# One TensorE loop for experts 4 to 30: the overflow branch moved from behind expert 15 to behind expert 3

## The chip, the cores and the metric

The kernel runs on one core of one Trainium2 chip. The metric is the device time of one execution in microseconds (us), as the median of several runs. The engines are called TensorE (PE), VectorE (DVE), ScalarE (ACT), GpSimd (POOL) and SyncE (SP). SyncE here only issues transfers and waits.

## The reference

One step of a hybrid decoder layer on 280 token rows (16 meta tokens, 256 prompt tokens, 8 sampled ones), all in float32. It has two sub-layers. The first mixes tokens (RG-LRU and gated linear attention) and isn't touched here. The second is a mixture of experts: 32 experts, of which each token takes 4. This is what the change is about:

```python
logits = u @ w_router + b_router
top_val, top_idx = lax.top_k(logits, TOP_K)          # 4 of 32
gates = softmax(top_val)
# for each expert e, on the rows routed to it:
gu = xb @ w_gu[e] + b_gu[e]                           # w_gu[e]: 1024 x 2048
gate = minimum(gu[:, :1024], 7.0)
lin = clip(gu[:, 1024:], -7.0, 7.0)
act = (lin + 1.0) * gate * sigmoid(1.702 * gate)
y += row_weight * (act @ w_down[e] + b_down[e])       # w_down[e]: 1024 x 1024
```

Each expert has 8.39 MB of `w_gu` and 4.19 MB of `w_down`, 12.58 MB in all and 402.7 MB for the 32. A final RMSNorm follows.

## The kernel before

**A pass.** Each expert is one pass (`body(i)` on every engine) over at most S = 64 rows that were routed to it. On TensorE a pass `i` does, in this order: the gate and up matmuls `gu(i, e, k0, k1)` in four quarters (L1560), with the scatter of the results of expert `i - 2` behind the second quarter (`scatter`, L1602) and the gather of the rows of expert `i + 1` behind the third (`gather`, L1532); the down matmuls of expert `i - 1` (`dn`, L1579); and a few transposes for what comes next (`turn_rows` L1539, `turn_weights` L1619, `turn_gu` L1626). VectorE and ScalarE do the activation of the expert before, copy results out of PSUM and add them to `yacc`.

**Counters.** The quarters increment `used0`, `used2`, `used4` and `used6` when their weights have been read, the four parts of `dn` increment `used8` to `used11`. `x_turned` is incremented when the rows of the next expert have been transposed, at the end of a pass.

**The weight queue.** All weights go through one ring of nine buffers of 2.1 MB each. SyncE issues the loads in order. For an expert from the fourth on there are two loads of `w_gu` of 4096 KB (`gate_linear_four`, for the pieces `GU[0]` and `GU[2]`) and the `w_down` of the expert before, as one load of 4096 KB (`down_whole`) or, for experts 0 to 2 and each third one after, as two of 2048 KB (`down`). Before each load it waits on two things: that the previous load of the same piece has landed (`landed`) and that TensorE has read what lies in the buffer (`used...`). For experts 3 to 15 this is `fours_ahead`: the first load waits for `used9 >= e - 2`, the second for `used0 >= e`. For experts 16 to 31 it is `fours_behind_rows`, which is the same but for the first load, which waits for `x_turned >= i`. `down_ahead` follows both. These loads run through the helper at L321 and have that line in the profile.

**Overflow.** If an expert gets more than 64 rows, more passes are needed. VectorE works out `flag` early, before the first pass ends. TensorE, VectorE, ScalarE and SyncE each read it once (`value_load`) and have a loop over EXTRA = 129 more passes under an `If`. With these inputs the flag is 0 and the loop is jumped over. Which expert the branch stands behind is `SPLIT`:

```python
    SPLIT = NE // 2        # 16
    BIAS = 2
```

TensorE runs experts 0 to 3 unrolled, a loop of 4 rounds with 3 unrolled passes each (experts 4 to 15), the flag and the jump over the overflow loop (also 3 unrolled passes long), a loop of 5 rounds with 3 passes (experts 16 to 30), and `finish` with expert 31. VectorE and ScalarE do the same through `passes`, with loops of one pass. SyncE's program is unrolled for all experts, but for the overflow loop. GpSimd has no part in the experts.

Of the kernel before, what the change touches and what calls it, by code (L numbers as in the profile page):

```python
# [5 lines left out]
def hybrid_layer_kernel(nc, A, O):  # L6
# [20 lines left out]
    NE, FF = A["w_gu"].shape[1], A["w_down"].shape[2]  # L27
# [21 lines left out]
    NSLOT = 18  # L49
    EXTRA = NV - NE + 1  # L50
    GU = list(range(0, 8, 2))
    SPLIT = NE // 2
    BIAS = 2
    DN = list(range(8, 12))
    DOWN = DN[::2]
    QUADS = range(BIAS + 1, NE)

    ctx = ExitStack()
    with ctx:
        sems = {}  # L60

        def sem(name):

            if name not in sems:
                sems[name] = ctx.enter_context(nc.semaphore(name))
            return sems[name]
# [211 lines left out]
        def four_of(e, p):  # L278

            n = (e * 6 + 7 + p // 2) % (NSLOT // 2)  # L280
            return mem[:, n * 4096:(n + 2) * 4096]
# [5 lines left out]
        def split_down(e):  # L287

            return e <= BIAS or e % 3 == 0

        def second_halves(e):

            return sum(split_down(j) for j in range(e + 1))

        def both_of(e):

            n = (e * 6 + 8) % (NSLOT // 2)
            return mem[:, n * 4096:(n + 2) * 4096]
# [5 lines left out]
        def e_of(i):  # L304
            return i if isinstance(i, int) else i % NE
# [13 lines left out]
        def _(sp):  # L319
            def load(dst, src, name):  # L320
                sp.dma_start(dst, src).then_inc(sem(name), 16)  # L321
# [49 lines left out]
            def gate_linear(p, i, e):  # L371

                first, k = p - p % 4, p % 4
                src = A["w_gu"][0, bass.ds(e_of(i), 1), first * P:(first + 4) * P, :].rearrange("e (p k) n -> p (e k) n", p=P)
                load(pair_of(e, p).rearrange("p (k n) -> p k n", k=2), src[:, k:k + 2, :], f"piece_in{p}")

            def gate_linear_four(p, i, e):

                src = A["w_gu"][0, bass.ds(e_of(i), 1), p * P:(p + 4) * P, :].rearrange("e (p k) n -> p (e k) n", p=P)
                load(four_of(e, p).rearrange("p (k n) -> p k n", k=4), src, f"piece_in{p}")  # L380

            def down_rows_of(i):

                return A["w_down"][0, bass.ds(e_of(i), 1), :, :].rearrange("e (p k) n -> p (e k) n", p=P)

            def down(p, i, e):

                k = 2 * (p - 8)
                load(down_of(e, p).rearrange("p (k n) -> p k n", k=4), down_rows_of(i)[:, k:k + 4, :], f"piece_in{p}")

            def down_whole(i, e):

                load(both_of(e).rearrange("p (k n) -> p k n", k=KD), down_rows_of(i), f"piece_in{DN[0]}")

            def landed(p, n):

                sp.wait_ge(sem(f"piece_in{p}"), 16 * n)
# [8 lines left out]
            gate_linear(GU[3], 1, 1)  # L406
            down(DN[0], 0, 0)
            sp.wait_ge(sem("used0"), 1)
            down(DN[2], 0, 0)
            sp.wait_ge(sem("u2_ready"), 3)  # L410
# [3 lines left out]
            def down_ahead(i, e, triples=0):  # L414

                landed(DN[0], i - 1)
                if not split_down(e - 1):
                    sp.wait_ge(sem("used4"), i)
                    down_whole(i - 1, e - 1)
                    return  # L420
                sp.wait_ge(sem("used2"), i)
                down(DN[0], i - 1, e - 1)
                landed(DN[2], triples + second_halves(e - 2))
                sp.wait_ge(sem("used4"), i)
                down(DN[2], i - 1, e - 1)

            def fours_ahead(e):

                landed(GU[0], e)
                sp.wait_ge(sem("used9"), e - 2)  # L430
                gate_linear_four(GU[0], e, e)
                landed(GU[2], e)
                sp.wait_ge(sem("used0"), e)
                gate_linear_four(GU[2], e, e)
                down_ahead(e, e)

            def ahead(e):

                landed(GU[0], e)
                sp.wait_ge(sem("used2" if e == 2 else "used6"), 1 if e == 2 else e - 1)  # L440
                gate_linear(GU[0], e, e)
                landed(GU[1], e)
                sp.wait_ge(sem("used4" if e == 2 else "used9"), 1 if e == 2 else e - 2)
                gate_linear(GU[1], e, e)
                landed(GU[2], e)
                sp.wait_ge(sem("used6" if e == 2 else "used11"), 1 if e == 2 else e - 2)
                gate_linear(GU[2], e, e)
                landed(GU[3], e)
                sp.wait_ge(sem("used0"), e)
                gate_linear(GU[3], e, e)  # L450
                down_ahead(e, e)

            def fours_behind_rows(i, e, triples):

                landed(GU[0], i)
                sp.wait_ge(sem("x_turned"), i)
                gate_linear_four(GU[0], i, e)
                landed(GU[2], i)
                sp.wait_ge(sem("used0"), i)
                gate_linear_four(GU[2], i, e)  # L460
                down_ahead(i, e, triples)
# [12 lines left out]

            ahead(2)
            for e in range(QUADS[0], SPLIT):
                fours_ahead(e)
            sp.wait_ge(sem("flag_ready"), 1)
            over = sp.value_load(flag[0:1, 0:1], min_val=0, max_val=1)
            with sp.If(over):  # L480
                with sp.Fori(0, EXTRA // 3) as g:
                    for f in range(3):
                        in_turn(g * 3 + (SPLIT + f), SPLIT + f)
            more = over * EXTRA
            extra_triples = over * (EXTRA // 3)
            for e in range(SPLIT, NE):
                fours_behind_rows(more + e, e, extra_triples)
            sp.wait_ge(sem("scattered"), TC * (BIAS - 1))
            load(gfin, A["g_final"].rearrange("(a n) -> a n", a=1).broadcast_to([P, D]), "gfin_in")
            for w in range(4):  # L490
# [15 lines left out]
        def passes(eng, body, finish, after_bias=None):  # L506

            body(0)
            body(1)
            body(BIAS)  # L510
            if after_bias is not None:
                after_bias()
            with eng.Fori(BIAS + 1, SPLIT) as i:
                body(i)
            eng.wait_ge(sem("flag_ready"), 1)
            over = eng.value_load(flag[0:1, 0:1], min_val=0, max_val=1)
            with eng.If(over):
                with eng.Fori(SPLIT, SPLIT + EXTRA) as i:
                    body(i)
            more = over * EXTRA  # L520
            with eng.Fori(SPLIT, NE - 1) as i:
                body(i + more)
            finish(more + (NE - 1))
# [4 lines left out]
        def lags(i):  # L528

            n = i if isinstance(i, int) else NE  # L530
            return n >= 1, n >= 2
# [714 lines left out]
        def _(pe):  # L1246
# [358 lines left out]
            def scatter(i, e):  # L1605
# [3 lines left out]
                pe.wait_ge(sem("biased"), 2 * i)  # L1609
                if e == BIAS + 1:  # L1610
                    pe.wait_ge(sem("gd_ready"), 2)
# [23 lines left out]
            def body(i, e, triples=0):  # L1635
                do_j, do_m = lags(e)

                pe.wait_ge(sem("xT_ready"), i + 1)
                if do_j:
                    pe.wait_ge(sem("guS_ready"), i)  # L1640
                gu(i, e, 0, 2)
                gu(i, e, 2, 4)
                if do_m:
                    scatter(i, e)
                gu(i, e, 4, 6)
                if do_m:
                    pe.wait_ge(sem("added"), TC * (i - 2) + 2)
                gather(i + 1)
                gu(i, e, 6, 8)
                if do_j:  # L1650
                    pe.wait_ge(sem("act_ready"), i)
                    if do_m:
                        pe.wait_ge(sem("added"), TC * (i - 1))
                    for p in DN:
                        dn(i, e, p, actT, 4, triples + second_halves(e - 1))
                turn_rows(i + 1)
                if do_j:
                    turn_weights(i, 6)
                if e == BIAS:
                    turn_gates()  # L1660
                if not do_j:
                    pe.wait_ge(sem("flag_ready"), 1)
                turn_gu(i)
# [29 lines left out]
                pe.wait_ge(sem("sq_h"), len(nth_half) + 2)  # L1693
                pe.matmul(ps[:, 1, 0:1], same_row, ssq[:, 2:3], start=True, stop=True).then_inc(sem("last_sum"), 1)

            for e in range(BIAS + 2):
                body(e, e)
            with pe.Fori(0, (SPLIT - BIAS - 2) // 3) as g:
                for f in range(3):
                    body(g * 3 + (BIAS + 2 + f), BIAS + 2 + f, g * 1)  # L1700
            pe.wait_ge(sem("flag_ready"), 1)
            over = pe.value_load(flag[0:1, 0:1], min_val=0, max_val=1)
            with pe.If(over):
# [3 lines left out]
            more = over * EXTRA  # L1707
            extra_triples = over * (EXTRA // 3)
# [30 lines left out]
```

## Time and profile before

| | |
|---|---|
| median of 3 runs | 1085.46 us (1085.46 to 1085.59) |
| the profiled execution | 1085.73 us, span of its instructions 1084.0 us |
| TensorE matmul | 97% of the span busy, mean granted clock 0.995 |
| VectorE, ScalarE | 30% and 18% |
| moved by DMA | 425.59 MB, mean 393 GB/s |

The span is the time from the first to the last instruction on the core, and the little around it belongs to the launch. A view of the profile can be restricted to a window, counted in microseconds from the start of the span. In the window view there is one row per window: its length, the busy time and the number of instructions of each engine, then the granted clock of TensorE (1.00 is full speed), the mean busy share of the 16 DMA engines (which can be a little over 1 by the way packets fall on borders) and GB/s. The chain of waits is followed back from the last instruction, each step to what released it.

In the trace, expert 0 starts on TensorE at 162.54 us, expert 3 at 234.75, expert 4 at 265.48 and expert 16 at 605.98.

### The profile page before, as it was taken

To read this page: it belongs to the slowest core of one execution; us is meant where nothing else is said; L and a number is where in the kernel's file an instruction comes from. 1 tells how busy PE (TensorE), PEld (TensorE's weight loads), DVE (VectorE), ACT (ScalarE), POOL (GpSimd) and SP (SyncE) were. 2 spreads that over 40 slices of the span, in tenths; PEclk is the share of its full clock that TensorE was granted. 3 is DMA by queue.
4 is the path that set the end of the run, shared out by engine and by line. 5 is a ranking of instruction groups with operands and counts; after the bars stand their busy time and mean duration, and the time that the engine had idled before them with its cause. 6 is when DMAs were issued, how large, how long until landed. Compare 5 with 4: busy or idle time off the path is not lost.

```text
span 1084.0 us, 13426 instructions
## 1 busy us (share of the span) xinstructions
PE 1051.5 (97%) x5387; PEld 436.1 (40%) x5387; DVE 325.2 (30%) x660; ACT 193.8 (18%) x319; POOL 14.9 (1%) x39
## 2 busy tenths in 40 slices
PE   7999999999999999999999799999999999999996
PEld 5758573333333333333333233333333333333332
DVE  6854342212222222222222222222222222122234
ACT  3463332111111111111111011111111111110112
POOL 4100000000000000000000000000000000000000
PEclk9999999999999999999999899999999999999999
DMA  9751689999999999999999999999999999999993
GB/s 303 262 192 50 253 360 386 425 427 414 433 429 428 435 433 424 438 432 430 433 428 433 430 427 432 430 432 433 426 435 432 429 432 434 432 429 432 435 406 148
DMA packets 34586, 425.59 MB, mean 393 GB/s; under 512 B 5335, under 2 KB 12334, under 8 KB 19450
## 3 DMA queue, kind: packets, MB, share of 16 engines
q1 hardware_dynamic: 33816, 424.76, 93.2%
q8 instruction: 22, 0.36, 0.1%
q0 software_dynamic: 512, 0.26, 0.1%
q10 hardware_dynamic: 226, 0.13, 0.0%
q14 instruction: 10, 0.08, 0.0%
HBM read 422.82 MB, written 2.35 MB: 392 GB/s over the span
## 4 chain that ended last, share of the span: by engine, by line
PE 62%; DMA 36%; issue 1%; DVE 1%; ACT 0%; SPq 0%; ACTq 0%; DVEq 0%
DMA mem<-in_w_gu 35%; PE ps L1560 24%; PE ps L1579 12%; PE ps L1278 6%; PE ps L1532 4%; PE ps L1602 3%; PE ps L1437 3%; PE ps L1626 2%; PE ps L1324 1%; PE ps L1539 1%; DMA mem<-in_w_in 1%; PE ps L1586 1%; PE ps L1619 1%; PE ps L1462 0%; PE ps L1317 0%
## 5 line engine op out<-in xcount | busy, mean ns | idle before, releaser
L1560 PE MATMUL ps<-mem 128*64 128x512 f32 x2048 | 459.8, 597 | 13.3 <-issue 6.3
L1560 PEld LDWEIGHTS ps<-mem 128*64 128x64 f32 x2048 | 141.9, 137 | 288.6 <-issue 272.8
L1579 PE MATMUL ps<-mem 128*64 128x512 f32 x1024 | 226.0, 593 | 0.7
L1170 DVE TENSOR_TENSOR mem<-ps,bguT 128x512 f32<-128x512 f32 x64 | 41.2, 686 | 372.6 <-PE ps L1626 372.6
L1579 PEld LDWEIGHTS ps<-mem 128*64 128x64 f32 x1024 | 75.3, 137 | 145.1 <-issue 145.0
L1200 DVE TENSOR_TENSOR yacc<-ps,yacc 128x1024 f32<-128x1024 f32 x64 | 75.6, 1220 | 131.1 <-PE ps L1602 131.1
L752 ACT ACTIVATE mem<-ps 128x512 f32<-128x512 f32 x32 | 19.1, 597 | 385.6 <-PE ps L1532 384.7
L1532 PE MATMUL ps<-mem 128*64 128x512 f32 x372 | 85.1, 592 | 0.0
L1278 PE MATMUL ps<-mem 128*128 128x280 f32 x256 | 64.4, 410 | 2.1 <-DMA mem<-in_w_in 2.1
L1602 PE MATMUL ps<-mem 64*128 64x512 f32 x256 | 64.1, 616 | 1.7 <-ACT mem L817 0.9
L1152 DVE TENSOR_TENSOR mem<-slot_no,pos 128x192 f32<-128x192 f32 x32 | 11.5, 358 | 165.9 <-PE ps L1532 165.9
L1278 PEld LDWEIGHTS ps<-mem 128*128 128x128 f32 x256 | 49.2, 194 | 14.9 <-DMA mem<-in_w_in 2.4
L803 ACT ACTIVATE mem<-ps 128x512 f32<-128x512 f32 x31 | 18.5, 597 | 179.7 <-PE ps L1579 179.5
L796 ACT ACTIVATE mem<-ps 128x1024 f32<-128x1024 f32 x32 | 32.8, 1024 | 99.4 <-PE ps L1560 99.4
L1532 PEld LDWEIGHTS ps<-mem 128*64 128x64 f32 x372 | 26.7, 137 | 53.1 <-issue 53.1
L1602 PEld LDWEIGHTS ps<-mem 64*128 64x128 f32 x256 | 21.9, 186 | 42.3 <-issue 42.3
L781 ACT ACTIVATE mem<-mem 128x512 f32<-128x512 f32 x30 | 18.9, 630 | 96.7 <-DVE mem L1177 96.7
L1626 PE MATMUL ps<-ident,mem 128*128 128x128 f32 x256 | 33.8, 275 | 0.5 <-ACT mem L796 0.5
L1626 PEld LDWEIGHTS ps<-ident,mem 128*128 128x128 f32 x256 | 30.9, 191 | 1.5 <-ACT mem L796 0.8
L1437 PE MATMUL ps<-mem 128*128 128x512 f32 (+1 forms) x80 | 28.9, 512 | 0.0
L1539 PEld LDWEIGHTS ps<-ident,mem 128*128 128x128 f32 x128 | 17.9, 209 | 25.2 <-issue 25.2
L1184 DVE TENSOR_SCALAR mem<-slot_no,pos,gate 128x128 f32<-128x128 f32 x96 | 27.3, 341 | 1.3 <-PE ps L1619 1.3
(318 smaller groups left out, 517.4 us busy)
## 6 DMA issues: line engine op xcount, KB each, us to landing
mem<-in_w_gu SPq DMA_DIRECT2D x58, 4096.0 KB, 27.5
mem<-in_w_down SPq DMA_DIRECT2D x18, 4096.0 KB, 29.0
mem<-in_w_down SPq DMA_DIRECT2D x26, 2048.0 KB, 24.2
mem<-in_w_gu SPq DMA_DIRECT2D x12, 2048.0 KB, 12.6
mem<-in_w_in SPq DMA_DIRECT2D x5, 2048.0 KB, 16.2
mem<-in_w_out SPq DMA_DIRECT2D x1, 4096.0 KB, 14.0
mem<-in_w_down SPq DMA_DIRECT2D x4, 1024.0 KB, 21.5
mem<-in_state_gla SPq DMA_DIRECT2D x8, 128.0 KB, 2.5
```

What stands on the lines that cost most here:

```text
L796: act.activation(guS[:, :].rearrange("p (a n) -> p a n", a=2), ps[:, 0:2, :], ACT.Copy).then_inc(sem("guS_ready"), 1)
L1170: dve.tensor_tensor(hS[:, n, :].rearrange("p (k s) -> p k s", k=8), turned[:, n], bguT[:, 8 * n:8 * n + 8, bass.ds(e_of(i - 1), 1)].broadc ...
L1184: dve.tensor_scalar(Gm[:, c, :], slot_no[:, :], pos[:, c, bass.ds(i - 1, 1)], gate[:, c, bass.ds(e_of(i - 1), 1)], ALU.is_equal, ALU.mult) ...
L1200: dve.tensor_tensor(dst, ps[:, PAIR[c]:PAIR[c] + 2, :], dst, ALU.add).then_inc(sem("added"), 1)
L1278: last = pe.matmul(ps[:, bank_of(t), 0:NT], w(k), uT[:, k, :], start=(k == K_ORDER[0]), stop=(k == K_ORDER[-1]))
L1437: last = pe.matmul(ps[:, OUT_BANK[c, n], 0:(k1 - k0) * P], mixed(k)[:, c * P:c * P + P], wout[:, k, k0 * P:k1 * P], start=(k == 0), stop=( ...
L1532: last = pe.matmul(ps[S * w:S * w + S, 5, :], sel[:, c, :], u2[:, c, w * 512:(w + 1) * 512], start=(c == 0), stop=(c == TC - 1))
L1539: last = pe.transpose(ps[:, 5, q * P:(q + 1) * P], xr[:, q:4 * P:4], ident[:, :])
L1560: last = pe.matmul(ps[S * w:S * w + S, n, :], xT[:, k % 4, k // 4, :], weights[:, col:col + 512], start=(k == 0), stop=(k == KD - 1))
L1579: last = pe.matmul(ps[S * w:S * w + S, bank, :], acts[:, k, :], weights[:, col:col + 512], start=(k == 0), stop=(k == KD - 1))
L1602: last = pe.matmul(ps[:, PAIR[c] + n, :], weights[S * n:S * n + S, c * P:(c + 1) * P], values[S * n:S * n + S, :], start=start, stop=stop)
L1626: last = pe.transpose(ps[:, 2 + f // 4, (f % 4) * P:(f % 4 + 1) * P], guS[:, f:KD * P:KD], ident[:, :])
```

## The change

- `SPLIT` becomes `BIAS + 2`, that is 4. The flag is read, and the overflow loop jumped over, behind expert 3 instead of behind expert 15, on SyncE, TensorE, VectorE and ScalarE.
- TensorE's loop over experts 4 to 15 is gone. What was the loop over 16 to 30 now covers 4 to 30, in 9 rounds of 3.
- VectorE and ScalarE run expert 3 unrolled, and then one loop over 4 to 30.
- SyncE keeps the waits that it had for each expert: `fours_ahead` up to expert 15 and `fours_behind_rows` from 16. As the experts from 4 on now lie behind the branch, `fours_ahead` takes a pass number `i` that comes from a register, beside the expert's number `e`, and its first two waits are exchanged.

```diff
--- before.py
+++ after.py
@@ -49,8 +49,8 @@
     NSLOT = 18
     EXTRA = NV - NE + 1
     GU = list(range(0, 8, 2))
-    SPLIT = NE // 2
     BIAS = 2
+    SPLIT = BIAS + 2
     DN = list(range(8, 12))
     DOWN = DN[::2]
     QUADS = range(BIAS + 1, NE)
@@ -424,15 +424,15 @@
                 sp.wait_ge(sem("used4"), i)
                 down(DN[2], i - 1, e - 1)
 
-            def fours_ahead(e):
-
-                landed(GU[0], e)
-                sp.wait_ge(sem("used9"), e - 2)
-                gate_linear_four(GU[0], e, e)
-                landed(GU[2], e)
-                sp.wait_ge(sem("used0"), e)
-                gate_linear_four(GU[2], e, e)
-                down_ahead(e, e)
+            def fours_ahead(i, e, triples=0):
+
+                sp.wait_ge(sem("used9"), i - 2)
+                landed(GU[0], i)
+                gate_linear_four(GU[0], i, e)
+                landed(GU[2], i)
+                sp.wait_ge(sem("used0"), i)
+                gate_linear_four(GU[2], i, e)
+                down_ahead(i, e, triples)
 
             def ahead(e):
 
@@ -474,7 +474,7 @@
 
             ahead(2)
             for e in range(QUADS[0], SPLIT):
-                fours_ahead(e)
+                fours_ahead(e, e)
             sp.wait_ge(sem("flag_ready"), 1)
             over = sp.value_load(flag[0:1, 0:1], min_val=0, max_val=1)
             with sp.If(over):
@@ -484,7 +484,10 @@
             more = over * EXTRA
             extra_triples = over * (EXTRA // 3)
             for e in range(SPLIT, NE):
-                fours_behind_rows(more + e, e, extra_triples)
+                if e < NE // 2:
+                    fours_ahead(more + e, e, extra_triples)
+                else:
+                    fours_behind_rows(more + e, e, extra_triples)
             sp.wait_ge(sem("scattered"), TC * (BIAS - 1))
             load(gfin, A["g_final"].rearrange("(a n) -> a n", a=1).broadcast_to([P, D]), "gfin_in")
             for w in range(4):
@@ -510,8 +513,7 @@
             body(BIAS)
             if after_bias is not None:
                 after_bias()
-            with eng.Fori(BIAS + 1, SPLIT) as i:
-                body(i)
+            body(BIAS + 1)
             eng.wait_ge(sem("flag_ready"), 1)
             over = eng.value_load(flag[0:1, 0:1], min_val=0, max_val=1)
             with eng.If(over):
@@ -1693,11 +1695,8 @@
                 pe.wait_ge(sem("sq_h"), len(nth_half) + 2)
                 pe.matmul(ps[:, 1, 0:1], same_row, ssq[:, 2:3], start=True, stop=True).then_inc(sem("last_sum"), 1)
 
-            for e in range(BIAS + 2):
+            for e in range(SPLIT):
                 body(e, e)
-            with pe.Fori(0, (SPLIT - BIAS - 2) // 3) as g:
-                for f in range(3):
-                    body(g * 3 + (BIAS + 2 + f), BIAS + 2 + f, g * 1)
             pe.wait_ge(sem("flag_ready"), 1)
             over = pe.value_load(flag[0:1, 0:1], min_val=0, max_val=1)
             with pe.If(over):
```

## Rows read from the trace of the kernel before

**Rows 1.** The page: rate in 40 slices of 27.1 us; one load's landing.

```profile
GB/s 303 262 192 50 253 360 386 425 427 414 433 429 428 435 433 424 438 432 430 433 428 433 430 427 432 430 432 433 426 435 432 429 432 434 432 429 432 435 406 148
...
mem<-in_w_out SPq DMA_DIRECT2D x1, 4096.0 KB, 14.0
```

**Rows 2.** The chain of waits: start, us, what.

```profile
265.48 7.02 PE ps L1560 x32
...
599.72 6.25 issue
605.98 8.48 PE ps L1560 x32
...
663.15 3.61 PE ps L1560 x16
...
695.03 29.07 DMA mem<-in_w_gu
...
1044.88 7.09 PE ps L1560 x32
```

**Rows 3.** Busy time by window, from 271 us on.

```profile
271.00:325.00 54.00, 54.00 (x272) 19.81 (x270) 13.81 (x25) 7.63 (x12) 0.00 (x0) 1.00 1.01 432
595.00:649.00 54.00, 47.75 (x236) 17.61 (x234) 14.14 (x25) 6.01 (x10) 0.00 (x0) 0.94 1.01 430
811.00:1000.00 189.00, 182.88 (x906) 67.36 (x906) 46.11 (x82) 24.54 (x38) 0.00 (x0) 1.00 1.00 431
```

**Rows 4.** L321: issues in 250 to 252, 259 to 270, 598.7 to 612.

```profile
L321 SPq DMA_DIRECT2D mem<-in_w_down x1: 328/328/328, 250.8 to 250.8; - x1
...
DMA to landing us min/median/max: 13.1/13.1/13.1
...
L321 SPq DMA_DIRECT2D mem<-in_w_gu x2: 328/328/328, 260.2 to 269.2; - x2
...
DMA to landing us min/median/max: 15.2/15.6/15.9
...
L321 SPq DMA_DIRECT2D mem<-in_w_gu x2: 332/332/333, 598.8 to 611.3; - x2
...
DMA to landing us min/median/max: 25.3/26.7/28.1
```

**Rows 5.** Busy time in the window from 606 to 609 us.

```profile
606.00:609.00 3.00, 3.00 (x8) 1.00 (x10) 0.00 (x0) 0.00 (x0) 0.00 (x0) 0.53 1.02 431
```

**Rows 6.** Instruction packets in 244 to 600, then in 600 to 690 us.

```profile
q8 instruction: 5, 0.08, 0.1%
...
q8 instruction: 5, 0.08, 0.4%
```

**Rows 7.** The timeline of SyncE's issues: start, us, what.

```profile
213.68 6.40 SPq L321 DMA_DIRECT2D mem<-in_w_down  x2
229.18 0.33 SPq L321 DMA_DIRECT2D mem<-in_w_gu  x1
...
278.66 0.33 SPq L321 DMA_DIRECT2D mem<-in_w_down  x1
...
588.16 1.01 SPq L321 DMA_DIRECT2D mem<-in_w_down  x2
```

**Rows 8.** L321: issues at 154.0 and 154.4 us, then at 166.2.

```profile
L321 SPq DMA_DIRECT2D mem<-in_w_gu x1: 328/328/328, 154.0 to 154.0; - x1
L321 SPq DMA_DIRECT2D mem<-in_w_down x1: 434/434/434, 154.4 to 154.4; - x1
...
DMA to landing us min/median/max: 7.4/9.7/11.9
...
L321 SPq DMA_DIRECT2D mem<-in_w_down x1: 328/328/328, 166.2 to 166.2; - x1
...
DMA to landing us min/median/max: 8.8/8.8/8.8
```

**Rows 9.** Waits in 596 to 608 us: total, times, longest.

```profile
ACT mem L781 <- DVE mem L1177: 3.4, 1, 3.4
```

## The prediction

> **What bounds the kernel now.** I read the page first. Its slices show the DMA at 360 GB/s by 135 us, then 425 and 427, a dip to 414 in the tenth slice (244 to 271 us), and from there never under 424 until the slice in which the last weights land [rows 1]. TensorE is busy 97% too, so the page alone doesn't say which of the two sets the end.
>
> Next the chain of waits [rows 2]. Up to 663 us it runs through TensorE (an expert every 27.85 us, one with the gap at 599.72 excepted), then through transfers of `w_gu`, one every 29.1 us. The tempting reading is that TensorE is the bound until 663 us and that every microsecond taken from it there is a microsecond won. The windows say otherwise [rows 3]: from 271 us on, in the TensorE part of the chain as in the DMA part, the rate is 429 to 434 GB/s with a share of 1.00 or 1.01 (eleven windows, of which three are shown). An expert is 12.58 MB (4.19 MB in each of three loads), at 431 GB/s 29.2 us. The DMA has been the bottleneck since 271 us. TensorE, at 27.85 us, only eats up a lead of landed weights, 1.3 us of it per expert, and at 663 us the lead is gone. The end is therefore: the moment from which the DMA never runs dry, plus the bytes left, plus the tail of TensorE work after the last landing at 1044.88 us. A TensorE stall costs nothing if the transfers already issued outlast it; otherwise what the DMA loses is never given back.
>
> So the measure is the backlog: for each load, how long after its issue the load before it lands. From the issues and their times to landing [rows 4]: at 611.3 us the previous load (598.8 + 28.1) lands at 626.9, a backlog of 15.6 us. At 269.2 us it (260.2 + 15.2) lands at 275.4: 6.2 us. At 260.2 us it (250.8 + 13.1) lands at 263.9: 3.7 us.
>
> **What the change removes: the stall at expert 16.** Between experts 15 and 16 TensorE stands 6.25 us for "issue" [rows 2]. There the program reads the flag, jumps over the unused overflow loop and enters the second loop. After it the granted clock is at half speed (1.2 GHz instead of 2.4) until about 609 us, with the engine idle before [rows 5]; the first 32 matmuls take 8.48 us where those of expert 4 take 7.02 [rows 2]. In all, the quarter that lets SyncE issue the next `w_gu` load comes 611.3 - 599.72 = 11.6 us after the expert's start, at expert 4 269.2 - 265.48 = 3.7 us: a delay of 7.8 us (some 0.1 of it SyncE's register work). The backlog there is 15.6 us, delay included, and the load issued at 611.3 lands at 636.6, 9.7 us after its predecessor, the full rate. The window around it, 430 GB/s [rows 3], agrees. So the term for the removal is **0**; its cover is the backlog.
>
> **What it adds: the same stall at expert 4.** Today TensorE falls straight into the first loop there, with no gap: the chain has its matmuls from 265.48 us on with no "issue" ahead of them [rows 2]. After the change the flag read and the jump over three unrolled overflow bodies stand at this place. Would the code already be in the engine? Five instruction packets come in 244 to 600 us, for twelve experts, and five in 600 to 690, for three [rows 6]: the first loop's code stays in the engine after its first round, and the code past the jump doesn't come ahead of the jump. The code jumped over is as long as the loop, so the target is as far off at expert 4 as it was at 16. I take the same delay, 7.8 us. Bounds: nothing, if it is hidden, and 7.8 us as measured; between them 4.5 us, if the fetch takes only the 2.5 us of latency that a quiet DMA shows below, with 2 us for the clock and the rest.
>
> The Trainium skill (Runtime: NRT & Kernel Launch, "Instruction fetch mechanics") says that an engine streams code in 16 KiB blocks and that a taken branch to a block outside what it holds stalls for a fetch by DMA. The rows of packets agree. Under it the stall moves whole and the sum is as below.
>
> **What lies behind it.** Everything SyncE issues after 265 us waits on TensorE's counters: the second `w_gu` half of expert 5 at 269.2 waits for `used0`, the `w_down` load at 278.7 [rows 7] for `used4`. The first would come at 269.2 + 7.8 = 277.0. The DMA runs dry at 275.4. What a load costs on a dry queue I bound by rows. A 2 MB load issued at 154.0 into a quiet DMA lands after 7.4 us, one issued at 166.2, just as its predecessor (154.4 + 11.9) ends, after 8.8 us [rows 8]. Less 4.85 us for 2.1 MB at full rate that is 2.55 and 3.95 us of latency, so 12.3 to 13.7 us for 4.2 MB; `w_out`, alone in its time, took 14.0 [rows 1], and the load at 260.2, on a backlog of 3.7 us, even 15.2. I take 13.7, the row in which the queue runs dry just then as here. The landing moves from 285.1 to 277.0 + 13.7 = 290.7, **5.6 us** later. Floor: 4.2 (with 12.3); with the short stall of 4.5 us, 0.9 to 2.3. Ceiling: 7.1 (with 15.2). The next load, `w_down`, moves from 278.7 to 286.5, 4.2 us before 290.7, so it follows nearly without a gap. At that backlog the load at 260.2 lost 11.5 - 9.75 = 1.75 us, so up to 1.7 may come on top until the backlog has grown. After that the DMA is never dry again and the loss stays to the end.
>
> The Trainium skill (DMA: Bandwidth & Descriptors) puts the fixed cost of a transfer near 2 us. The rows here show 2.5 to 4.3; by the page's figure the term would be 277.0 + 11.7 - 285.1 = 3.6 us instead of 5.6, an estimate.
>
> **The rest.** SyncE's own branch moves to between 219.7, when the second `w_down` half is issued (the pair that begins at 213.68 and lasts 6.40), and 229.18 us, when it goes on [rows 7]: it stands 9.1 us for `used9` there. At expert 16 its branch fitted between the `w_down` issues that begin at 588.16 and end at 589.2, and the issue at 598.8, 9.6 us [rows 4, 7], without being seen. I take 0. Where it needs more than the 9.1, a backlog of at least 3.7 us (the thinnest, rows 4) covers the first part; what is beyond that is lost one for one, and I allow 3 us for it. ScalarE's branch lies in a wait of 3.4 us ended by VectorE's data [rows 9], VectorE's in a longer one: 0. If ScalarE's cover were gone, the excess would delay the activation, which TensorE wants only behind all its gate and up matmuls. The exchanged order of `used9` and the landed wait changes nothing, as both must hold: 0. Register values in twelve experts' waits and addresses: 0.1 us an issue, under a backlog of 6 us and more: 0. Unrolling expert 3 on ScalarE and VectorE: same work, same waits, 0.
>
> **Sum.** 0 + 5.6 + 0 = 5.6 us. The profiled execution took 1085.73 (span 1084.0), the median is 1085.46, so the sum on the former is 1091.3 and on the median **1091.1 us**, half a per cent slower.
>
> **Rivals.**
> (a) *The queue runs dry* as worked out: 1088.5 to 1093.2. For it: 6.2 us of backlog against 7.8 of delay. Chance 0.64.
> (b) *The stall is hidden or short.* A delay under some 4.5 us is absorbed but for 2 us, and the time is 1085.5 (1084.5 to 1087.5). For it: a DMA with little queued may bring the code faster than the full one at 600 us. Against it: the packets are there only after the jump in the one case shown. Chance 0.20.
> (c) *SyncE falls late as well.* From 9.1 us plus at least 3.7 of backlog on, each microsecond of its branch is one more on top of (a): with up to 3 of them 1091.1 to 1094.1. For it: its branch is only known to fit into 9.6 us at expert 16, where nothing would have shown a late issue of some microseconds, with 15.6 of backlog. Chance 0.08.
> (d) *Faster.* The chain is right to go through TensorE, and what counts is its time up to 663 us. The branch, now close behind the start of the loop code, costs no more than the fall into the loop does today: 7.8 us go and none comes back, 1085.5 - 7.8 = 1077.7. It decides only if the rate can rise above 431 GB/s once TensorE frees its buffers sooner. The windows of rows 3 speak against it, the backlog of 15.6 us too. Chance 0.08.
>
> **Numbers.** Within 0.2% (2.2 us) is what a measurement can't tell from no change. (a) and (c) lie outside it: slower 0.72; (b) 0.20; (d) 0.08. The likeliest case alone: 1088.5 to 1093.2. The range takes in (b) from 1085.2 and (a) to 1093.2; it leaves out (d), the worse part of (c) and a little of (b).
>
> **What the next profile would show.** A gap for "issue" of about 6 us on TensorE near 265 us, with a half clock behind it, and none near 600; instruction packets there and none later. The load that waits for `used0` of expert 4 is issued near 277 us and lands near 290.7. The window 250 to 290 us shows a hole of 5 to 6 us' worth of bytes, the later windows 431 GB/s as before. The chain turns from TensorE to transfers earlier than 663 us, since the landings are then 5.6 us later than now, and TensorE, behind the place of the old branch, no later. I am wrong if the gap is shorter than 4 us, or if a load in a dry queue lands as fast as one behind another.

## The result: 0.71% slower

The change takes 1093.62 us (median of 6 runs, 1090.97 to 1095.56) against 1085.46 (6 runs, 1084.88 to 1086.3): 8.2 us more, ratio 1.0071, interval [1.0061, 1.0081]. The sign and the mechanism are those forecast. The median lies 2.5 us over the predicted 1091.1 and 0.4 us over 1093.2, the top of the range, which is less than the uncertainty of the measured difference (about 1.1 us either way).

The page of the changed kernel, the rate in 40 slices (27.3 us each), the answer to [rows 1]:

```profile
GB/s 312 264 178 47 273 358 364 421 428 424 306 431 425 438 428 433 431 436 428 433 431 431 431 432 431 427 434 430 427 436 434 430 434 429 433 428 433 430 414 149
```

Nearly all of the difference is in one slice, the eleventh (273 to 300 us): 306 GB/s. Behind it the rate is what it was. The chain of waits shows why, and where it now turns to transfers (start, us, what; compare [rows 2]):

```profile
265.88 0.89 PE ps L1628 x8
266.77 6.01 issue
272.78 9.13 PE ps L1562 x32
...
553.43 3.61 PE ps L1562 x16
...
557.23 28.64 DMA mem<-in_w_gu
...
1052.60 7.09 PE ps L1562 x32
```

The gap for "issue" has moved whole, from 599.72 to 266.77 us, and the matmuls behind it are slow (9.13 us instead of 7.02). The chain enters the transfers at 557 us instead of 667, and the last landing is at 1052.60, 7.7 us later than before. By window (the columns are those of [rows 3]):

```profile
262.00:268.00 6.00, 4.77 (x29) 2.49 (x25) 1.01 (x2) 1.58 (x3) 0.00 (x0) 1.00 1.03 423
268.00:274.00 6.00, 1.22 (x4) 0.54 (x6) 3.19 (x8) 0.63 (x1) 0.00 (x0) 0.67 0.86 362
274.00:280.00 6.00, 6.00 (x22) 1.72 (x20) 0.00 (x0) 0.00 (x0) 0.00 (x0) 0.76 0.28 76
280.00:286.00 6.00, 6.00 (x34) 1.90 (x32) 2.68 (x3) 0.00 (x0) 0.00 (x0) 1.00 0.88 371
286.00:292.00 6.00, 6.00 (x30) 2.01 (x28) 0.36 (x1) 0.60 (x1) 0.00 (x0) 1.00 0.96 399
292.00:300.00 8.00, 8.00 (x40) 2.73 (x38) 0.00 (x0) 1.02 (x1) 0.00 (x0) 1.00 0.96 391
```

Read the last two columns downwards. TensorE stands still from 267 to 273 us, and the DMA runs dry some 8 us later, between 274 and 280 us: a share of 0.28 and 76 GB/s. While it is dry TensorE is busy again, so neither engine's own busy share shows the loss. The load that ends the hole, and the one behind it (line L321, issue and time to landing, as in [rows 4]):

```profile
L321 SPq DMA_DIRECT2D mem<-in_w_gu x1: 333/333/333, 278.7 to 278.7; - x1
...
DMA to landing us min/median/max: 12.2/12.2/12.2
...
L321 SPq DMA_DIRECT2D mem<-in_w_down x1: 333/333/333, 288.2 to 288.2; - x1
...
DMA to landing us min/median/max: 14.4/14.4/14.4
```

The predecessor (261.8 + 14.0) had landed at 275.8, 2.9 us before the issue at 278.7. The DMA was without work for longer than that, as finer windows of the change show:

```profile
271.00:273.00 2.00, 0.22 (x2) 0.23 (x4) 0.42 (x1) 0.00 (x0) 0.00 (x0) 0.50 0.88 377
273.00:275.00 2.00, 2.00 (x6) 0.55 (x6) 0.00 (x0) 0.00 (x0) 0.00 (x0) 0.50 0.15 57
275.00:279.00 4.00, 4.00 (x16) 1.19 (x14) 0.00 (x0) 0.00 (x0) 0.00 (x0) 0.76 0.00 0
279.00:281.00 2.00, 2.00 (x12) 0.69 (x10) 0.00 (x0) 0.00 (x0) 0.00 (x0) 1.00 0.98 262
```

A share of 0.15 is two or three of the 16 engines. Most of them had nothing left from 273 us on, 2.8 us before the load counts as landed, and no byte of the next load moves before 279 us. So the DMA stands nearly idle for some 6 us, not for 2.9: the landing of a load is not the moment up to which all engines have work. The next load lands at 302.6, 11.7 us behind the one at 290.9, where 9.7 is the full rate.

In this profiled execution everything from 158 us on is also 1.3 us late for a reason of its own: TensorE's clock was at half speed for a moment there (0.72 in the first row, of the change; 1.00 in the same window of before). Of the eleven others profiled below only e12's has it, so it isn't the change's.

```profile
156.00:162.00 6.00, 5.71 (x23) 2.18 (x22) 3.73 (x20) 3.07 (x4) 0.00 (x0) 0.72 0.99 426
```

### The profile page after: what moved, and what is told of

It reads as the page before. It is cut to its first block, busy times and chain, and to the rows that moved or that the text cites. A ratio compares the mean times of both kernels' runs of the same rounds, so it can differ in the third digit from the quotient of the medians.

```text
span 1092.0 us, 13490 instructions
## 1 busy us (share of the span) xinstructions
PE 1055.1 (97%) x5387; PEld 437.1 (40%) x5387; DVE 325.2 (30%) x660; ACT 193.8 (18%) x319; POOL 14.9 (1%) x39
## 4 chain that ended last, share of the span: by engine, by line
PE 51%; DMA 46%; issue 1%; DVE 1%; ACT 0%; SPq 0%; ACTq 0%; DVEq 0%
DMA mem<-in_w_gu 45%; PE ps L1562 19%; PE ps L1581 9%; PE ps L1280 6%; PE ps L1534 3%; PE ps L1439 3%; PE ps L1604 2%; PE ps L1628 1%; PE ps L1326 1%; DMA mem<-in_w_in 1%; PE ps L1541 1%; PE ps L1588 1%; PE ps L1621 0%; PE ps L1464 0%; PE ps L1319 0%
## 5 line engine op out<-in xcount | busy, mean ns | idle before, releaser
L1154 DVE TENSOR_TENSOR mem<-slot_no,pos 128x192 f32<-128x192 f32 x32 | 11.5, 359 | 167.7 <-PE ps L1534 167.0
L1280 PEld LDWEIGHTS ps<-mem 128*128 128x128 f32 x256 | 49.1, 194 | 14.6 <-DMA mem<-in_w_in 2.1
L1186 DVE TENSOR_SCALAR mem<-slot_no,pos,gate 128x128 f32<-128x128 f32 x96 | 27.3, 340 | 1.3 <-PE ps L1621 1.3
```

What stands on the lines that cost most here:

```text
L1186: dve.tensor_scalar(Gm[:, c, :], slot_no[:, :], pos[:, c, bass.ds(i - 1, 1)], gate[:, c, bass.ds(e_of(i - 1), 1)], ALU.is_equal, ALU.mult) ...
L1280: last = pe.matmul(ps[:, bank_of(t), 0:NT], w(k), uT[:, k, :], start=(k == K_ORDER[0]), stop=(k == K_ORDER[-1]))
```

## The experiments

**Theory.** The end is set by the microseconds in which the weight queue is dry (or nearly so); TensorE's stall behind expert 3 is longer than the backlog there. **Rivals:** the other engines' branches or SyncE's register waits; TensorE's time itself; the branch as such, wherever it stands.

### e1: no branch on TensorE

```diff
-            pe.wait_ge(sem("flag_ready"), 1)
-            over = pe.value_load(flag[0:1, 0:1], min_val=0, max_val=1)
-            with pe.If(over):
...
+            over = 0
```

> The changed kernel without TensorE's flag read and overflow loop (left out: overflow passes on TensorE; with these inputs they never run). SyncE, VectorE and ScalarE keep their branches behind expert 3 and SyncE its register waits. Theory (only TensorE's stall costs): no gap on TensorE between experts 3 and 4, the w_gu load that waits for used0 of expert 4 issued 3.7 us after that expert's start, 1085.5 us, ratio to before 0.999 to 1.001. Rival 1 (SyncE's branch or its register waits cost part of the 8 us): 1087.5 us or more. Rival 2 (TensorE's time up to 663 us counts): the stall is gone from everywhere, 1077.7 us.

Measured: 1084.51 us, ratio to before 0.9987 [0.9977, 0.9996]. All 8 us are gone, with SyncE's, VectorE's and ScalarE's branches and the twelve experts' register waits still at their new place. Rivals 1 and 2 fall: those parts cost nothing that can be told from 0, and removing TensorE's stall doesn't give 7.8 us on top.

### e2: the flag read kept, the jump made short

```diff
             with pe.If(over):
-                with pe.Fori(0, EXTRA // 3) as g:
-                    for f in range(3):
-                        body(g * 3 + (SPLIT + f), SPLIT + f, g * 1)
+                pe.wait_ge(sem("flag_ready"), 1)
+                pe.wait_ge(sem("flag_ready"), 1)
```

> The changed kernel, TensorE's flag read and branch kept behind expert 3, but the branch jumps over two waits instead of three unrolled passes (left out: overflow passes on TensorE). Theory (the stall is a code fetch of a far jump): the gap shrinks from 6.0 to under 2.5 us, the queue doesn't run dry (backlog 6.2 us), 1085.5 to 1086.5 us. Rival (the stall is the flag read or the branch itself): the gap stays 6 us and the time is that of the change, 1091 to 1095 us.

Measured: 1084.42 us, 0.9990 [0.9981, 1.0]. The chain of waits of e2 at the place of the gap:

```profile
265.28 0.89 PE ps L1628 x8
266.16 7.02 PE ps L1562 x32
```

There is no gap at all and the clock stays up. So the flag read and a taken branch are free here, and the 6 us belong to the distance jumped, that is to the three unrolled passes that lie between.

### e3 and e12: the branch behind expert 6, and behind expert 9

```diff
-    SPLIT = BIAS + 2
+    SPLIT = BIAS + 5        # e12: BIAS + 8
```

with TensorE's first loop (one round, in e12 two) and that of `passes` in front of the branch as in the kernel before.

> The changed kernel with the branch behind expert 6 (SPLIT = 7) on all engines, experts 4 to 6 as one round of a first loop. In the trace of before the load that waits for used0 of expert 7 is issued at 352.7 us, its predecessor (343.8 + 20.6) lands at 364.4. Theory (backlog against delay): the stall of 6 us is there in full, the issue comes 7.8 to 8.2 us later, 3.5 to 3.9 us before the queue runs dry; no dry queue, at most the 1.7 us that a thin backlog cost before: 1085.5 to 1087.2 us. Rival 1 (the longer second loop or the register waits cost, wherever the branch stands): most of the 8 us stays, over 1090 us. Rival 2 (TensorE's time counts): 1085.5 us, and the changed kernel's loss would be unexplained.

> The changed kernel with the branch behind expert 9 (SPLIT = 10) on all engines. Before, the load that waits for used0 of expert 10 is issued at 436.3 us on a backlog of 15.6 us; with the 8 us of the stall 7 to 8 us are left, over the 6 us under which loads lost time. Theory (backlog against delay): 1085.5 us, between 1084.5 and 1086.5, with the stall of 6 us on TensorE in full. Rival (the branch costs in proportion to how early it stands, without a threshold; 8.2 us at 4, 3.0 at 7): still 1 to 2 us over before, 1086.5 to 1087.5.

Measured: behind expert 6 1088.43 us, 1.0033 [1.0021, 1.0044]; behind expert 9 1085.85 us, 1.0001 [0.999, 1.0011]. The stall is there both times (the chain of waits, first e3, then e12):

```profile
348.62 6.94 issue
```

```profile
433.89 6.00 issue
```

| branch behind expert | backlog at its load in before, us | issue of that load, its backlog now | over before |
|---|---|---|---|
| 3 | 6.2 | 278.7, -2.9 | 8.2 us |
| 6 | 11.7 | 361.2, 1.7 | 3.0 us |
| 9 | 15.6 | 445.8, 6.8 | 0.2 us, not told from 0 |

(Backlog is the landing of the load before, less the issue, both from L321's rows: in e3 343.6 + 19.3 - 361.2 = 1.7, in e12 428.9 + 23.7 - 445.8 = 6.8.) The cost follows the backlog. The rival without a threshold asked for 1 to 2 us at expert 9; the measured difference of 0.2 us has an interval of about -1.1 to 1.2 us, so that only its lower edge is left. The windows there, first of e3, then of e12, say the same:

```profile
358.00:360.00 2.00, 2.00 (x10) 0.64 (x8) 0.00 (x0) 0.00 (x0) 0.00 (x0) 0.70 0.76 320
360.00:362.00 2.00, 2.00 (x12) 0.68 (x10) 0.00 (x0) 0.00 (x0) 0.00 (x0) 1.00 0.13 49
```

```profile
434.00:450.00 16.00, 10.11 (x38) 3.23 (x40) 4.21 (x9) 0.63 (x1) 0.00 (x0) 0.79 1.02 434
```

In e12 the DMA never falls off. In e3 I expected no dry queue and at most 1.7 us, and got 3.0. The gap was 0.9 us longer, and the expectation took the landing of the load before (362.9) as the time up to which the DMA is busy. It is nearly idle from 360 us on, although the issue at 361.2 comes 1.7 us before that landing. So the threshold isn't a backlog of 0 but of some microseconds. By their landings the loads of e3 took 11.0, 11.7, 10.4, 10.2 and 10.6 us, among others of 9.7, between 352 and 425 us. The bytes are lost before 380 us: 390 GB/s in 340 to 380 us (before: 430), 430 GB/s in 380 to 420.

### e5: the same lateness from work, without a branch

```diff
+                for _ in range(8 if isinstance(i, int) and i == BIAS + 1 else 1):
-                for f in range(8):
-                    last = pe.transpose(...)
+                    for f in range(8):
+                        last = pe.transpose(...)
```

> The kernel before (branch behind expert 15), with the 8 transposes at the end of expert 3's pass on TensorE done 8 times: 56 more of them, 7 x 0.89 = 6.2 us of work at full clock, at the place where the change puts the stall. Theory (any lateness of TensorE there dries the queue): the load issued at 269.2 comes at 275.4, just as the queue runs dry, and lands at 275.4 + 12.2 = 287.6 instead of 285.1, 2.5 us late; with up to 3.4 us more behind it, as in the changed kernel: 1088 to 1091.5 us. Rival (it is the far branch with its code fetches, not the place): 1085.5 us.

Measured: 1090.02 us, 1.0042 [1.0027, 1.0058], inside the forecast. The chain of waits, and L321's load behind it:

```profile
265.19 7.14 PE ps L1627 x64
272.33 7.02 PE ps L1560 x32
```

```profile
L321 SPq DMA_DIRECT2D mem<-in_w_gu x1: 327/327/327, 276.0 to 276.0; - x1
...
DMA to landing us min/median/max: 12.2/12.2/12.2
```

TensorE is busy the whole time, at full clock, with its usual code, and 4.4 us are lost. The place and the lateness decide, not the branch. The time to landing on a dry queue is 12.2 us again. Here too the DMA is idle well before the landing of the load before, at 275.7 us, and the issue comes only 0.3 us behind that landing:

```profile
272.00:274.00 2.00, 2.00 (x11) 0.77 (x12) 1.48 (x3) 0.00 (x0) 0.00 (x0) 1.00 0.24 90
274.00:276.00 2.00, 2.00 (x12) 0.72 (x10) 1.90 (x6) 0.54 (x1) 0.00 (x0) 1.00 0.00 0
```

### e6: no branch anywhere, the term of the removal

The flag reads and overflow loops of all engines are taken out of the kernel before (`over = 0`, as in e1, on each).

> The kernel before with the flag reads and overflow loops taken out on all engines (left out: overflow passes, which never run with these inputs). Prediction's term for the removal of the stall at expert 16: 0, so 1085.5 us, 1084.9 at the least. Rival (the stall at 16 costs about a microsecond after all, as 1084.5 us without it in the first two experiments suggests): 1084.5 us. Second rival (TensorE's time counts): 1077.7 us.

Measured: 1083.96 us, 0.9990 [0.998, 0.9999]. The predicted term is 0 and the measured one about 0.1%, 1 us, and at most 0.2%, 2 us. The trace doesn't put it at expert 16: the load that is issued at 436 us lands at 459.1 in e6 and at 461.6 in before, so the lead of 2.5 us is there long before the old branch, and at the last landing (1042.85 against 1044.88) it is 2.0. Between these two executions it comes from loads before 350 us that landed late in before; why they did so isn't shown. Whether the median's 1 us belongs to the stall stays open.

### e7 and e8: two versions that keep the whole function

In e7 TensorE's overflow passes are further rounds of the same loop. The passes are numbered through in any case, so no code has to be jumped over:

```diff
-            with pe.If(over):
...
-            with pe.Fori(0, (NE - 1 - SPLIT) // 3) as g:
+            with pe.Fori(0, extra_triples + (NE - 1 - SPLIT) // 3) as g:
                 for f in range(3):
-                    body(more + g * 3 + (SPLIT + f), SPLIT + f, extra_triples + g)
+                    body(g * 3 + (SPLIT + f), SPLIT + f, g * 1)
```

e8 adds to it `SPLIT = 7` with experts 0 to 6 unrolled on the compute engines, and the bias matmuls one stage later:

```diff
+    LATE = 6
-                if e == BIAS + 1:
+                if e == LATE:
                     pe.wait_ge(sem("gd_ready"), 2)
-                if e == BIAS:
+                if e == LATE - 1:
                     turn_gates()
```

> The changed kernel with nothing left out: TensorE's overflow passes are more rounds of the same loop, whose number of rounds is worked out from the flag, so no branch jumps over them; the other engines as in the change. Theory (only the far jump costs): no gap near 266 us, the time of the kernel without TensorE's branch, 1084.5 us (ratio to before 0.998 to 1.000). Rival (a loop bound from a register costs at each round, nine of them): a gap at each third expert, 1086 us or more, if the queue gets dry early on.

> As the last, with experts 0 to 6 unrolled and the bias matmuls (2.9 us of TensorE work) in the pass of expert 6 instead of 3. Theory (what sets the end is the microseconds in which the queue is dry or thin before about 300 us): expert 4 starts 2.9 us sooner, the loads behind expert 3 are issued sooner, the backlog of 3.7 us before the first load of expert 5 becomes 5 us or more and the 1.75 us lost there are won: 1082.5 to 1084 us. Rival (that loss comes from the code packet that passes in it, not from the thin queue): it is lost elsewhere, 1084.5 us.

Measured: e7 1084.86 us, 0.9994 [0.9985, 1.0003]; e8 1083.91 us, 0.9986 [0.9977, 0.9995]. e7 has the whole function and no gap (its transposes end and the matmuls of expert 4 begin at 265.6 us). It equals the kernel before. By its ratio e8 is 1.5 us faster than before, and by the medians 9.7 us faster than the change. Its first load of expert 5 is issued at 256.1 us on a backlog of 7.4 us and takes 9.7, where in before it came at 260.2 on 3.7 and took 11.5. The intervals of e7 and e8 overlap, so it isn't shown that the late biases alone give something.

### e9, e10, e11: does a thin queue lose time by itself?

All three are e7 with the transposes of `turn_gu` repeated in each pass from expert 4 on (twice in e9 and e10, three times in e11), e9 also with e5's eight times at expert 3. One execution each.

> What is open: in the changed kernel the loads behind the dry one took up to 11.7 us instead of 9.7, 3.5 us lost in all, while the backlog was under 6 us; the slow ones are those in which a 16 KB instruction packet passed. This is the one-loop kernel with the 8 transposes at the end of expert 3's pass done 8 times (the queue runs dry once) and those at the end of every later pass done twice (0.89 us more per pass, 28.74 us against the 29.1 of the DMA, so the backlog grows by only 0.4 us per expert and stays under 8 us until past 600 us). No instruction packets come after the first round of the loop (about 360 us). Theory A (a thin queue loses time only when an instruction packet passes): from 370 us on every load takes 9.7 us. Theory B (a thin queue loses time by itself): losses of 0.4 to 2 us go on at a backlog of 3 to 6 us, one or more per expert, until it has grown over 6.

> As the last, without the padding in expert 3's pass: the queue doesn't run dry, the backlog stays between 5 and 9 us until past 600 us. Theory A: no load after 370 us takes more than 9.8 us (4.9 for the halves), the time is that of the one-loop kernel, 1083 to 1086 us. Theory B: losses go on through the experts, 1087 us or more.

> The last two didn't decide: their backlog was 7 us and more from 370 us on. Now the transposes at the end of each pass behind expert 3 are done three times (a pass takes 27.85 + 2 x 0.89 = 29.6 us, more than the DMA's 29.1), so the backlog shrinks by 0.5 us per expert, from some 6 us at expert 7 to under 3 at expert 13 and on, with no instruction packet between 370 us and the end. TensorE sets the time here, some 1115 us. Theory A (a thin queue loses time only when an instruction packet passes): loads take 9.7 us as long as the backlog is over some 3 us. Theory B (a thin queue loses by itself): loads of 10.1 to 11.7 us, about one in three, from a backlog of 6 us downwards.

Measured: e9 1098.57, e10 1092.32, e11 1117.73 us. e10's time missed its expectation, by an error of mine: at 28.74 us a pass TensorE never eats up its lead and sets the end itself, as its window shows, 189.00 us busy of 189.00 where it was 182.88 in before [rows 3]:

```profile
811.00:1000.00 189.00, 189.00 (x964) 71.93 (x964) 50.73 (x91) 24.10 (x38) 0.00 (x0) 1.00 1.00 432
```

e9 and e10 didn't decide the question, as their backlog rose to 7 us and more from about 350 us on (6.2 to 6.7 us at the first loads behind expert 15), and no load was slow there. e11 did. The DMA queues of e11 in 372 to 1000 us have no row for TensorE's code (q8):

```profile
q1 hardware_dynamic: 10125, 265.72, 99.8%
q14 instruction: 3, 0.02, 0.0%
```

and yet a load like this one (L321) took 10.5 us, 0.8 too many, its predecessor having landed at 459.8, on a backlog of 3.7:

```profile
L321 SPq DMA_DIRECT2D mem<-in_w_down x1: 332/332/332, 456.1 to 456.1; - x1
...
DMA to landing us min/median/max: 14.2/14.2/14.2
```

Between 370 and 580 us, at backlogs of 3.3 to 4.2 us, five of thirteen loads took 10.1 to 10.5 us and the other eight 9.7 or 9.8; at 4.3 us and more none was slow. From expert 16 on the first load of each expert but the last few came at about 2 us (one at 0.3) and landed 12.1 to 12.5 us after its issue, which is the dry queue's time. So theory A falls in its strict form: under 4.3 us a thin queue can lose 0.4 to 0.8 us by itself, and at 2 us a load behaves as on a dry queue. This agrees with the windows above: the change's DMA had run out 2.8 us before the landing, and the next bytes came no sooner than 0.3 us behind the issue. Theory B fails as well as it was put, from 6 us downwards. The later landings at 4.5 us and over (0.7 and 1.2 us at a backlog of 4.7 in e11 near 300 and 320 us, 1.5 at 5.7 in the change) are all from the first round of a loop, when code is being fetched. That the packets cause them was argued from their times, not tried alone.

## Why the prediction was right, and what was mis-sized

**Right.** DMA-bound since 271 us, the chain's TensorE part no proof of the contrary: e1 and e6 have no 6 us of TensorE stall in the chain and are only about 1 us faster than before. The stall moves whole (6.01 us, in e3 6.94, in e12 6.00), and e2 ties it to the far jump. The Trainium skill (Runtime: NRT & Kernel Launch, "Instruction fetch mechanics") says that a taken branch to code outside what the engine holds waits for a fetch, and these runs agree. The packets of code come in the first window and not in the second (DMA queues in 244 to 600 us; in 600 to 690 the row of q8 is missing; compare [rows 6]):

```profile
q8 instruction: 6, 0.10, 0.1%
```

SyncE's branch costs nothing (e1), so rival (c) is out. Rival (b) needed a delay under 4.5 us, and it is 8.0 (below). Rival (d) is out by e1.

**The dry load.** 5.6 us predicted, 5.6 measured. That the two agree so well is luck, as two terms were off by 1.5 and 1.3 us and cancel. Against e6, the same kernel without branches, in which the two loads are issued at 260.2 and 269.1 us and the second takes 14.6 us to land: the delay is (278.7 - 261.8) - (269.1 - 260.2) = 8.0 us (7.8 predicted), the dry queue's time to landing 12.2 us (13.7 taken; the quiet-DMA row of [rows 8] had it right), and 8.0 + 12.2 - 14.6 = 5.6. My 15.9 for the undisturbed landing, where e6 has 14.6, held a loss of its own, from the slow load in front. Over four kernels a load on a dry queue lands 12.1 to 12.5 us after its issue, 2.4 to 2.8 of it beyond the 9.7 of transfer. The Trainium skill (DMA: Bandwidth & Descriptors, "Anatomy of one DMA — SWDGE (gpsimd) path") has a fixed cost of about 2.0 us, fitted to transfers that GpSimd issues. By it the landing would come after 11.7 us, an estimate; these loads are SyncE's, and the measured value is 0.4 to 0.8 us higher.

**The mis-sized term.** It is the sentence "so it follows nearly without a gap", with up to 1.7 us "on top" that I left out of the sum. The loads behind the hole, from L321's rows (took = from landing to landing):

| load | change: issue, backlog, took | e6: issue, backlog, took |
|---|---|---|
| w_gu second, expert 5 | 278.7, -2.9, 15.1 | 269.1, 5.0, 9.6 |
| w_down, expert 4 | 288.2, 2.7, 11.7 | 278.6, 5.1, 9.7 |
| w_gu first, expert 6 | 297.7, 4.9, 9.7 | 288.0, 5.4, 10.1 |
| w_gu second, expert 6 | 306.6, 5.7, 11.2 | 296.9, 6.6, 9.7 |
| w_down, expert 5 | 316.1, 7.5, 9.6 | 306.4, 6.8, 9.7 |
| sum of took | 57.3 | 48.8 |

8.5 us in all: 5.5 in the dry load, 3.0 in the four behind it. With 3.0 instead of 0 the sum is 8.6 us, and the measured difference to before 8.2 (e6 is about 1 us faster than before, so against it the five loads leave some of the difference over). The same showed in e5 (12.5 and 11.2 us for the two loads at and behind the dry moment) and e3.

Landing times tell how much was lost, but not when the DMA lost it. The rate does; first the change, then before:

```profile
270.00:280.00 10.00, 7.22 (x24) 2.25 (x26) 1.33 (x4) 0.60 (x1) 0.00 (x0) 0.66 0.47 173
280.00:290.00 10.00, 10.00 (x54) 3.24 (x52) 2.68 (x3) 0.00 (x0) 0.00 (x0) 1.00 0.89 380
290.00:300.00 10.00, 10.00 (x50) 3.40 (x48) 0.36 (x1) 1.62 (x2) 0.00 (x0) 1.00 0.98 395
300.00:330.00 30.00, 30.00 (x155) 11.56 (x152) 7.25 (x13) 4.97 (x9) 0.00 (x0) 1.00 1.01 431
```

```profile
270.00:280.00 10.00, 10.00 (x52) 3.19 (x50) 2.75 (x4) 0.00 (x0) 0.00 (x0) 1.00 1.01 431
280.00:290.00 10.00, 10.00 (x50) 3.32 (x48) 0.36 (x1) 1.62 (x2) 0.00 (x0) 1.00 0.99 426
290.00:300.00 10.00, 10.00 (x55) 4.26 (x51) 4.21 (x9) 2.19 (x4) 0.00 (x0) 1.00 1.00 428
300.00:330.00 30.00, 30.00 (x149) 10.88 (x147) 7.94 (x14) 3.82 (x6) 0.00 (x0) 1.00 1.01 433
```

At 431 GB/s the missing bytes are 6.0, 1.1, 0.8 and 0.1 us of work, 8.0 in all. So three quarters are lost in the hole itself, and next to nothing behind 300 us. The 1.9 us between 280 and 300 us fit a queue that is still thin, as the load at 288.2 is issued on a backlog of 2.7 us. The load that landed at 323.5, 1.5 us later than at the full rate, did so while the DMA moved 433 GB/s; one packet of code passed in that time (the change in 312 to 324 us, then the DMA queues in 313 to 324):

```profile
312.00:324.00 12.00, 12.00 (x64) 4.08 (x58) 1.92 (x4) 1.62 (x2) 0.00 (x0) 1.00 1.01 433
```

```profile
q8 instruction: 1, 0.02, 0.6%
```

So behind the mis-sized term stands the step "The DMA runs dry at 275.4". It took the landing of the load before as the end of its transfers, and priced what lies behind the dry load at nothing. Most engines ran out at 273 us, the hole was some 6 us, and 2 us more went just behind it. In 250 to 290 us the forecast hole of 5 to 6 us was 6.5 us (349 GB/s, 419 in before). The bounds show the same gap. By its own floor and ceiling (4.2 and 7.1 us) rival (a) would span 1089.7 to 1092.6 us, and with the 1.7 us "on top" reach 1094.3, which holds the result; the range stated for it, 1088.5 to 1093.2, isn't worked out.

**The removal.** 0 predicted; measured 0 to 2 us by e6, about 1 us. Its place wasn't found.

## What to carry to other kernels

When a stream of transfers sets the end, ask of each stall not how long it is but how much issued work lies behind it at that moment: landing of the load before, less the issue. The same stall of 6 to 7 us cost 8.2, 3.0 and 0 us at backlogs of 6, 12 and 16 us. Take off some 3 to 4 us of the backlog before you trust it as cover (an estimate from the 2.8 us in the change's windows and from e11, whose losses end at 4.3), as the DMA runs out of bytes before the last load counts as landed. How much work the DMA lost, and when, is read from its rate in fine windows, not from the landings. Code for a rare case is best made more rounds of the loop that runs anyway; if it must be jumped over, do it where the queue is full.

## What the runs showed of the hardware

- A flag read from memory and a taken branch on TensorE are hidden altogether when the target is near (e2, no gap), and cost 6.0 to 6.9 us when it lies behind three unrolled passes, in a full DMA (e12, backlog of 15.6 before it) no more than in one with little queued (the change).
- A 4.19 MB load on a dry queue lands 12.1 to 12.5 us after its issue, on a full one 9.7 us after its predecessor. Between, at a backlog of 3.3 to 4.2 us, five loads of thirteen came 0.4 to 0.8 us late while TensorE fetched no code (e11), and at 2 us one lands as on a dry queue (12.1 to 12.5 us after its issue).
- The 16 DMA engines don't run out together: in the change all but two or three were idle 2.8 us before the load counted as landed (share 0.15 in 273 to 275 us), in e5 the share was 0.24 in 272 to 274 us and 0.00 in 274 to 276, with the landing at 275.7.
- Near code fetches loads landed 0.4 to 2.0 us late at backlogs of up to 8.3 us, and one 1.5 us late, in before, on 15 us. Such a late landing need not be work lost by the DMA: its rate was 433 GB/s in the change in 312 to 324 us, and 427 in before in 320 to 350.
- Behind the gap TensorE ran the next matmuls at half clock (0.67 and 0.76 granted in 268 to 274 and 274 to 280 us), which added 2.1 us to the 6.0.
